# Who makes the RWKV chain's new state: the decay of the old state on GpSimd and one VectorE operation, for an identity product on TensorE and a copy on ScalarE

## The reference

```
def _wkv_step(S, inp):
    r, k, v, w, kk, b = inp
    sa = jnp.einsum('bhij,bhj->bhi', S, -kk)
    S = S * w[:, :, None, :] + sa[..., None] * b[:, :, None, :] + v[..., None] * k[:, :, None, :]
    return S, jnp.einsum('bhij,bhj->bhi', S, r)
...
S_T, o = lax.scan(_wkv_step, S0.astype(f32), xs)
```

## Time and profile before

| | |
|---|---|
| median of 3 runs | 4096.57 us (4095.34 to 4099.92) |
| the profiled execution | 4089.57 us, span 4087.7 us |
| mean granted clock | 0.957 of full |
| TensorE busy | 3781.7 us (93%) |
| VectorE busy | 1935.2 us (47%) |
| ScalarE busy | 1445.9 us (35%) |
| GpSimd busy | 402.8 us (10%) |

### The profile page before, as it was taken

One profiled execution on the slowest core, in us unless ns is written; L12 is line 12 of the kernel. 1 busy time (PEld: TensorE's weight loads), 2 busy tenths in 40 slices (PEclk: granted clock), 3 DMA queues, 4 the chain that ended last, 5 costly groups with the idle time before them and its releaser, 6 DMA issues.

```text
span 4087.7 us, 93200 instructions
## 1 busy us (share of the span) xinstructions
PE 3781.7 (93%) x40189; PEld 3475.4 (85%) x40189; DVE 1935.2 (47%) x2605; ACT 1445.9 (35%) x2180; POOL 402.8 (10%) x556
## 2 busy tenths in 40 slices
PE   6968889999999989899999999999796888999999
PEld 5947785899999965599999999999794778499999
DVE  4375542455425654355533445542546554345532
ACT  2344441244322343344422234432233444134431
POOL 0011211011100000001100101110001212101100
PEclk8989997899999999999999999999898999699999
DMA  3200000122222358522222222222220000012222
GB/s 118 78 27 3 3 24 25 49 83 82 80 87 78 109 205 303 210 80 82 82 85 83 83 75 82 82 81 86 80 74 17 3 3 24 24 64 82 82 80 80
DMA packets 95927, 314.57 MB, mean 77 GB/s; under 512 B 18946, under 2 KB 20226, under 8 KB 94866
## 3 DMA queue, kind: packets, MB, share of 16 engines
q1 hardware_dynamic: 87410, 285.25, 20.7%
q10 hardware_dynamic: 8224, 24.88, 1.6%
HBM read 297.30 MB, written 12.79 MB: 76 GB/s over the span
## 4 chain that ended last, share of the span: by engine, by line
PE 83%; DVE 9%; ACT 6%; issue 1%; DMA 0%; ACTq 0%; SPq 0%; DVEq 0%
PE ps L401 21%; PE ps L403 20%; PE ps L402 20%; PE ps L1053 6%; DVE xt L746 2%; PE ps L1297 2%; PE ps L524 1%; DVE xl L740 1%; PE ps L1290 1%; PE ps L862 1%; PE ps L1327 1%; DVE a_zz L912 1%; PE ps L454 1%; PE ps L1610 1%; PE ps L875 1%
## 5 line engine op out<-in xcount | busy, mean ns | idle before, releaser
L401 PE MATMUL ps<-xh,wh 128*128 128x288 f32 x4976 | 1495.7, 301 | 74.8 <-DVE xl L740 73.3
L402 PE MATMUL ps<-xl,wh 128*128 128x288 f32 x4976 | 1471.6, 296 | 0.0
L403 PE MATMUL ps<-xh,wl 128*128 128x288 f32 x4976 | 1466.2, 295 | 0.0
L401 PEld LDWEIGHTS ps<-xh,wh 128*128 128x128 f32 x4976 | 936.2, 188 | 93.3 <-issue 51.2
L402 PEld LDWEIGHTS ps<-xl,wh 128*128 128x128 f32 x4976 | 937.8, 188 | 3.0
L403 PEld LDWEIGHTS ps<-xh,wl 128*128 128x128 f32 x4976 | 940.1, 189 | 0.0
L376 ACT ACTIVATE wh<-raw 128x1024 fp32r<-128x1024 f32 x415 | 439.2, 1059 | 1247.3 <-PE ps L403 1239.2
L383 DVE TENSOR_TENSOR wl<-raw,wh 128x1024 fp32r<-128x1024 f32 x415 | 508.2, 1225 | 622.6 <-ACT wh L376 621.9
L401 PE MATMUL ps<-hh,wh 128*128 128x288 f32 x1536 | 463.1, 302 | 0.0
L403 PE MATMUL ps<-hh,wl 128*128 128x288 f32 x1536 | 455.6, 297 | 0.0
L402 PE MATMUL ps<-hl,wh 128*128 128x288 f32 x1536 | 448.6, 292 | 0.0
(11 more groups left out here) (305 smaller groups left out, 4675.4 us busy)
## 6 DMA issues: line engine op xcount, KB each, us to landing
raw<-in_w SPq DMA_DIRECT2D x415, 512.0 KB, 3.2
kp<-in_cache_k SPq DMA_DIRECT2D x64, 512.0 KB, 5.5
vp<-in_cache_v SPq DMA_DIRECT2D x64, 512.0 KB, 6.2
rkv<-in_wkv ACTq DMA_DIRECT2D x2, 2048.0 KB, 9.3
out_wkvs<-rkv ACTq DMA_DIRECT2D x2, 2048.0 KB, 7.2
x<-in_x ACTq DMA_DIRECT2D x1, 2304.0 KB, 13.3
out_k<-qk ACTq DMA_DIRECT2D x1, 2304.0 KB, 7.1
out_v<-vg ACTq DMA_DIRECT2D x1, 2304.0 KB, 12.7
```

The source lines that it names most:

```text
L401: pe.matmul(out, w_h, rhs_h, start=(first and k == 0), stop=False)
L402: pe.matmul(out, w_h, rhs_l, start=False, stop=False)
L403: mm = pe.matmul(out, w_l, rhs_h, start=False, stop=(last and k == nk - 1))
```

## The change

The state in PSUM no longer holds the old state, so the product of line 1120 goes, and the sum starts with the product of line 1121. GpSimd multiplies the old state by the chunk's decay into a new buffer `sdec`, in part 1 of each g but the first. VectorE, in part 2, multiplies the PSUM sum by the decay and adds `sdec` in one operation (for g = 0 it only multiplies), and signals `a_s` in ScalarE's place. ScalarE keeps its copies to `xb`, `ust` and the output.

```diff
--- before.py
+++ after.py
@@ -206,6 +206,7 @@
         wkvo = at("wkvo", [KD, 64], F32, a.take(2048))
         w2s = at("w2s", [P], F32, a.take(512))
         scan0 = at("scan0", [TP], F32, a.take(4 * TP))
+        sdec = at("sdec", [64], F32, a.take(256))
         assert a.at <= misc
         a1 = Map(misc)
         spread16 = at("spread16", [16, 64], F32, a1.at)
@@ -276,6 +277,8 @@
                 "m e d qx qxt qX qxb qU qus qo qvq quq qs qad qmu "
                 "g gd gm gb gc gs gq gi gr gx gl ge row out").split())
 
+
+        a_sd = sem("a_sd")
 
         class Ph:
             pass
@@ -1116,9 +1119,7 @@
                 if g == 0:
                     after(pe, a_oe, B.cnt(1, 1))
                 for r in HEADS:
-                    if g:
-                        pe.matmul(s_[r], mview("ist")[r], was[r], start=True, stop=False)
-                    pe.matmul(s_[r], sl["ktok"][r, g], sl["vst"][r, g], start=(g == 0), stop=False)
+                    pe.matmul(s_[r], sl["ktok"][r, g], sl["vst"][r, g], start=True, stop=False)
                 for r in HEADS:
                     if g:
                         pe.matmul(out[r], was[r], sl["ar"][r, g, 1], start=True, stop=False)
@@ -1141,17 +1142,29 @@
                 act.wait_ge(a_cu, n)
                 act.activation(ust[:], bank(6, CT), ACT.Copy).then_inc(a_ue, 1)
             if part == 2:
-                act.wait_ge(a_cs2, n)
-                to = sst[:, (g + 1) % 2:(g + 1) % 2 + 1] if g < NCK - 1 else wkvo[:, B.at(0)]
-                act.activation(to, bank(5)[:, CT:2 * CT].unsqueeze(1), ACT.Copy, scale=sl["p"][:, g, CT - 1:CT])\
-                    .then_inc(a_s, 1)
                 if g == NCK - 1:
                     act.wait_ge(a_co, n)
                     act.activation(B.row(rkv, 0), bank(4).rearrange("p (c t) -> p c t", t=CT), ACT.Copy)\
                         .then_inc(a_oe, 1)
 
-        def no_chain(eng, B, g, part):
-            pass
+        def chain_dve(dve, B, g, part):
+            if part != 2:
+                return
+            n, end = B.tile(NCK, g + 1), slots[B.s]["p"][:, g, CT - 1:CT]
+            to = sst[:, (g + 1) % 2] if g < NCK - 1 else wkvo[:, B.c]
+            dve.wait_ge(a_cs2, n)
+            if g:
+                dve.wait_ge(a_sd, B.tile(NCK - 1, g))
+                dve.scalar_tensor_tensor(to, bank(5)[:, CT:2 * CT], end, sdec[:], ALU.mult, ALU.add).then_inc(a_s, 1)
+            else:
+                dve.tensor_scalar(to, bank(5)[:, CT:2 * CT], end, None, ALU.mult).then_inc(a_s, 1)
+
+        def chain_pool(pool, B, g, part):
+            if part != 1 or g == 0:
+                return
+            end = slots[B.s]["p"][:, g, CT - 1:CT]
+            pool.wait_ge(a_s, B.tile(NCK, g + 1))
+            pool.tensor_scalar(sdec[:], sst[:, g % 2], end, None, ALU.mult).then_inc(a_sd, 1)
 
 
         NSTEP = len(INV)
@@ -1409,14 +1422,14 @@
             a_norm_dve(dve, layer, j)
             mixes(dve, layer, j, mix_rows_dve, mix_chunk_dve)
             dve.wait_ge(s_mm, plan[layer, MIX[-1][0]].c0 + 1)
-            rwkv(dve, j, inv_dve, no_chain, prep_dve, seq_dve)
+            rwkv(dve, j, inv_dve, chain_dve, prep_dve, seq_dve)
             gn_dve(dve, j)
             res_dve(dve, plan[layer, "out"], 1, norm_behind(layer, "out"), in_place[layer])
 
         def a_pool(pool, layer, j):
             pool.wait_ge(s_mm, plan[layer, MIX[-1][0]].c0 + 1)
             pool.wait_ge(a_ld, 64 * (j + 1))
-            rwkv(pool, j, inv_pool, no_chain, prep_pool, seq_pool)
+            rwkv(pool, j, inv_pool, chain_pool, prep_pool, seq_pool)
 
 
         NQ = 2 * KD
```

## The result

The changed kernel takes 4112.12 us (median of 7 runs, 4108.22 to 4121.22); the kernel before, on the same chip, 4096.57 (7 runs, 4091.81 to 4099.92). The ratio is 1.0043, 95% interval 1.0033 to 1.0053: slower by 17.6 us (13.5 to 21.7) by this ratio, which takes in all runs, outside the 0.2% that a measurement tells.

What follows compares the result with a forecast made beforehand. TensorE sets most of a half, but VectorE's program order makes the state late. Seven full-clock halves at +1.05, seven slow-stretch at +0.48 and two short at -0.17 sum to +10.4 us: 4107.0, range 4092 to 4120.

Steps and rivals of the forecast that it cites:

- the clock rival: New waits near g=3 to g=5 bring half-clock stretches in seven halves more, 10.2 us: 4117; chance 0.14.
- (a): At g=1 VectorE takes the aak mask ahead of the state: +0.45 us, nothing lost in slow-stretch halves.
- (b): At g=2 ScalarE's copy, table load and sigmoid are the bound: net +0.01 us to the next product.
- (c): At g=3 and g=4 the state waits behind VectorE's scan, then line 897 and the RECIPROCAL: +1.11 us, the largest term.
- (d): At g=5 the state comes behind VectorE's line 907, which takes 1.79 us: +0.42 us.
- (e): At g=6 lines 910, 912 and the add precede the state, +0.44; line 875 waits less, -0.57: net -0.13 us.
- (f): g=6, g=7 and next inversion, VectorE free: identity products -0.24, hand-over -0.04, lines 919 and 922 -0.08: net -0.36 us.
- the short half: The half where chain 7 runs beside the sample batch, two in all: -0.17 us each, too small to matter.
- Slow-stretch half: Each of seven long halves with one 3.4 us stretch at half clock: 0.57 less than at full clock, +0.48 us.
- the race: If GpSimd's line 955 starts 0.02 us later, VectorE's line 907 takes 0.69 instead of 1.79: 4091.6; chance 0.08.
- Cheaper hand-overs: VectorE's state takes 0.21 us, giving back some 0.3 us a half: +6, 4102.5, no measurable change; chance 0.25.
- TensorE as the bound: VectorE reaches the state before TensorE needs it: -13.4 from products, some 3 us from ScalarE's relief: 4080; chance 0.11.

Runs made afterwards that it cites:

- state_before_scan: Changed kernel with only g=2's state moved ahead of the scan in VectorE's order; 4116.56 us, ratio 1.0046 to the kernel before.
- state_before_904: Changed kernel with only g=4's state moved ahead of lines 904 and 907 in VectorE's order; 4099.65 us, ratio 1.0011 to the kernel before.
- state_on_vector: Changed kernel with the identity product back and no decay on GpSimd, VectorE only scaling the PSUM sum; 4142.67 us, ratio 1.0106 to the kernel before.
- state_first: Changed kernel with states moved ahead of mask, scan, reciprocal product and step 13's add, RECIPROCAL split around g=3's state; 4065.42 us, ratio 0.9920 to before.
- no_identity_act: Kernel before with only the identity product left out, ScalarE still making the state; 4088.55 us, ratio 0.9982 to the kernel before.
- state_first_filled: state_first plus 16 unread TensorE products in the wait before line 865's second product; 4062.03 us, ratio 0.9928 to the kernel before.
- decay_unread: Kernel before with GpSimd's decay added, read by nobody, ScalarE waiting for it and making the state; 4099.33 us, ratio 1.0001 to the kernel before.
- no_reciprocal_after: Changed kernel with the RECIPROCAL replaced by a cheap operation writing a constant; 4089.43 us, ratio 0.9987 to the kernel before.
- split_reciprocal: Changed kernel with the RECIPROCAL cut in two and g=3's state between the parts; 4101.79 us, ratio 1.0018 to the kernel before.
- state_first_filled_twice: state_first_filled plus 8 and 14 more unread products before the last two inversion steps; 4058.20 us, ratio 0.9910 to the kernel before.

## Why the prediction was right

Forecast 4107.0, measured 4112.12: inside the range of 4092 to 4120, on the side that had the most chance, but just outside the forecast's own 4104 to 4111, and halfway to the 4117 of the clock rival. The sum was +10.4; measured 17.6 (13.5 to 21.7), so it was too small by some 7 us. Most of the mechanism was right, and one part of it, the clock, was not; that this part cost only 7 us is luck. Step by step, for a half at full clock:

| step | predicted | measured |
|---|---|---|
| (a) and (b), to g=2's next product | +0.01 | +0.02 |
| (c) scan, RECIPROCAL | +1.11 | +1.02 |
| (d) g=5 behind 910 | +0.42 | +0.44 |
| (e) g=6, with line 875 (878) | -0.13 | -0.03 |
| (f) to the next inversion | -0.36 | -0.13 |
| sum | +1.05 | +1.32 (1.33 by the windows) |

(a) to (d) stand, (a) by itself with +0.46 for +0.45, and the durations too: the operation that no row showed takes 0.26 to 0.28 us for the 0.27 taken. (TensorE's wait at g=4 was to be 0.6 us and is 0.25; g=4 opens at +5.87 from the add, for the 5.96 forecast.) *state_before_scan* and *state_before_904* show the cause by moving the state alone. They also show that an earlier opening is mostly lost again at the next: all of 1.11 us in the one, 1.60 of 2.07 in the other. (e) The lock of SBUF went as foreseen (0.68 and 0.69 us); line 878 starts 0.39 after 1111, not 0.24. The Trainium skill (SBUF — State Buffer, Who interferes with whom) tells of one shared pair of ports, which the engine that issues first holds for its whole instruction, and the traces agree: in *state_on_vector*, with 966 and 968 in front, 913 takes 1.66 us; in the changed kernel, where these come behind it, 0.68. (f) The two identity products gave their -0.24. The quicker hand-over booked at -0.04 did not come, and one term was missing: the state written to `wkvo` goes ahead of lines 922 and 925.

```profile
438.07 0.69 DVE L1085 TENSOR_TENSOR m<-ps,m 128x512 f32<-128x512 f32 x1 [0.75 <-PE ps L1056]
438.68 0.27 DVE L1158 SCALAR_TENSOR_TENSOR wkvo<-ps,p,sdec 128x64 f32<-128x64 f32 x1
438.87 0.68 DVE L922 SCALAR_TENSOR_TENSOR ar<-a_kraw,a_pprev 128x512 f32<-128x512 f32 x1
```

Line 922 starts 0.80 behind its add where line 919 started 0.61 behind its own, and 925 follows 0.08 sooner than 922 did, as booked. The next inversion's first product comes 0.11 later, where -0.08 was booked.

The decay at no cost stands; so does the small size of the short half (28.43, before 28.35), though not its sign.

The step that failed is "Slow-stretch half: 0.57 less, +0.48". It took for granted that the stretches at half clock keep their number and their place, though a changed number of them was one of the prediction's own signs of being wrong. In the trace after, the 12 intervals hold 11 of them, not 7: three at 11 to 13 us into the half, near the old place (9 to 10 us, and 12 in the half of c = 7), four at 3 us and, as the clock rival had it, four at 32 us, behind the wait of 1.85 us for g=5. Where one stayed in its place the discount is there: the half of c = 7 with one stretch went from 43.24 to 44.13, +0.89, which is 0.44 less than 1.33. But only three stayed, and those at 3 us cost 1.54 each (42.86 for 41.32), those at 32 us 1.02 (42.34).

The count, in the two profiled executions: the 12 intervals grew by 18.9 us, where the same steps gave 12 x 1.05 - 7 x 0.57 = 8.6. Of the 10.3 between, 12 x 0.28 = 3.4 are mostly terms (e) and (f), and 6.9 are the clock: 4.0 of discount that was booked, and 2.9 that the stretches cost more than before (13.3 us for 10.4). The spans differ by 25.4. The 6.5 outside the 12 intervals are 2 x 1.33 in the first long half of each layer, and 3.8 more. The granted clock is 0.957 before and 0.953 after, which is 352 and 387 us at half clock over the span, and the 12 intervals hold only 14 of these 35 us. One further stretch after the change stands in layer 3's first long half, at 3194; others stand where the change does nothing, as at 224.5 and 238.0, ahead of the first preparation. Which of them make up the 3.8 stays open. Part of this changes from run to run, as the 13 us between the lowest and the highest run of the changed kernel show. The ratio, which is over all runs, has 17.6 for 10.4.

There are three smaller faults in the working. The cut at line 1150 gives 12 long intervals and not 14, so what the first long half of each layer does was assumed. The time given for the race, 4091.6, lies outside the range from 4092 that was said to hold it. And a state of 0.19 us would by the prediction's own five hand-overs take 14 x 5 x 0.08 = 5.6 us off the sum, not some 4.

**The rivals.** Cheaper hand-overs is out: the operation took what was forecast. The clock was right in part: the wait for g=5 does bring stretches, in four halves for the seven that it took, at 1.02 us each for 1.46. The race was not won: GpSimd starts line 958 at 425.25, VectorE line 910 at 425.28, and that takes 1.79. TensorE as the bound did not come, but *state_first* shows its condition to be real: with VectorE's order rewritten, the RECIPROCAL and line 907 (now 910) out of the way among the rest, the same change is 31 us faster than before, more than the 17 that this rival gave it. *no_identity_act* shows that the 13.4 us of identity products which it counts are 7.4 in the order that the kernel has.

What stays open: which wait brings a stretch and which doesn't. The changed kernel's half from 396.99 has the same waits ahead of g=5 as the half before it and no stretch.

## What to carry to other kernels

An operation moved to a less busy engine can be late by what stands ahead of it in that engine's program, whatever the engine's load: here VectorE was busy for 54% of a half and late five times in it. Read for each dependent step what the new engine executes just before it, and write the order anew together with the move; here that, with the RECIPROCAL cut in two, made +0.4% into -0.8%. One such move alone may only shift the wait to the next step, so a first try that gains nothing doesn't refute the cause.

## What the runs showed of the hardware

In these traces TensorE's granted clock falls to half for stretches of 3.4 us, behind waits of at most 1.85 us each. Windows of the changed kernel: ahead of a stretch and in it; then the same waits in the next half, ahead of g=5 and behind.

```profile
382.00:385.30 3.30, 1.45 (x46) 1.31 (x43) 2.79 (x4) 2.28 (x4) 1.56 (x2) 0.98 0.00 0
385.30:388.60 3.30, 3.30 (x67) 3.30 (x66) 1.98 (x3) 0.45 (x2) 0.70 (x2) 0.50 0.02 5
```

```profile
425.30:428.60 3.30, 1.45 (x48) 1.31 (x46) 2.28 (x3) 1.57 (x4) 2.21 (x3) 1.00 0.00 0
428.60:431.90 3.30, 3.00 (x85) 2.72 (x82) 2.45 (x5) 1.04 (x3) 0.72 (x2) 1.00 0.02 5
```

The longest single wait of TensorE in either is 1.85 us. In the first case the clock is 1.2 GHz right behind, in the second it stays at 2.4, with TensorE busy for 1.45 us in both; what tells the two apart stays open. The Trainium skill (TensorE: Matmul & The Clock Gate, HAM oscillation — how this bites in real kernels) describes idling between groups of products, there in waits for a transfer, that lowers the clock again and again. The traces agree that the clock falls behind idling; here the waits are for VectorE and ScalarE and each is short, and *state_first_filled* removed the stretches behind the pause that it filled. A stretch costs 1.0 to 1.5 us here, so a kernel's time can move by some 10 us with how many fall into its halves (an estimate: 7 stretches more or less). In the profiled executions *decay_unread* lost its gain so, and *no_reciprocal_after*, *split_reciprocal* and *state_before_904*, with a stretch left in c = 7 alone, gained more than their shorter halves give. The unread products of *state_first_filled_twice* left none in the 12 intervals and cost nothing that a half shows (38.23 us for 38.22).

GpSimd's decay of 128 x 64 takes 0.44 us; in *state_first*, beside the scan that starts 0.18 us ahead of it, 1.58:

```profile
407.99 1.22 DVE L896 TENSOR_TENSOR_SCAN a_csum<-scan,a_zz 128x512 f32<-128x512 f32 x1
...
408.17 1.58 POOL L1170 TENSOR_SCALAR sdec<-a_sst,p 128x64 f32<-128x64 f32 x1 [4.89 <-DVE a_sst L1161]
```

It ends 0.54 us behind the end of the scan, which reads two SBUF tensors. So the small operation too was held by VectorE; here it still ended in time.
